# The opening of a two-block kernel: the loads on one queue with x between the conditioning pieces, the first norm's root one chunk earlier

## The reference

```
c_act = silu(c)
mod = c_act @ w_ada[l] + b_ada[l]            # 1024 x 6144
sh_m, sc_m, gt_m, sh_f, sc_f, gt_f = split(mod, 6)
h = rms_norm(x, g_pre_mix[l]) * (1.0 + sc_m) + sh_m
y = mixing_sublayer(h, cos, sin, w_in[l], ...)   # proj = h @ w_in, rotary q and k, attention, pool
```

## Time and profile before

| what | value |
|---|---|
| median of 3 runs | 1512.08 us |
| lowest, highest | 1511.72, 1513.73 us |
| the profiled execution's own time | 1513.09 us |
| its span in the trace | 1511.3 us |
| PE busy | 1467.7 us, 97% of the span |
| DVE, ACT, POOL busy | 41%, 43%, 48% |
| mean granted TensorE clock | 0.983 of full |

### The profile page before, as it was taken

One profiled execution on the slowest core, in us unless ns is written; L12 is line 12 of the kernel. 1 busy time (PEld: TensorE's weight loads), 2 busy tenths in 40 slices (PEclk: granted clock), 3 DMA queues, 4 the chain that ended last, 5 costly groups with the idle time before them and its releaser, 6 DMA issues.

```text
span 1511.3 us, 19773 instructions
## 1 busy us (share of the span) xinstructions
PE 1467.7 (97%) x7614; PEld 1229.0 (81%) x7614; DVE 623.3 (41%) x911; ACT 646.3 (43%) x941; POOL 718.7 (48%) x612
## 2 busy tenths in 40 slices
PE   8999999999999999999989989999999999999996
PEld 7899977888888888888956788888887888887885
DVE  6878456333332111522046311432456656553002
ACT  4453455545444322322255443553435555554331
POOL 3555215545454554555422363445546645455452
PEclk8999999999999999999999989999999999999998
DMA  8764133232322233235211232222322232323321
GB/s 350 279 245 159 30 97 107 84 109 86 101 93 83 81 115 95 73 111 140 98 42 57 84 111 84 84 84 84 112 84 84 83 111 83 111 77 98 95 85 65
DMA packets 27963, 160.77 MB, mean 106 GB/s; under 512 B 4824, under 2 KB 5080, under 8 KB 13176
## 3 DMA queue, kind: packets, MB, share of 16 engines
q1 hardware_dynamic: 25248, 151.08, 29.0%
q10 hardware_dynamic: 2648, 8.75, 2.1%
HBM read 157.04 MB, written 2.78 MB: 106 GB/s over the span
## 4 chain that ended last, share of the span: by engine, by line
PE 69%; issue 10%; DVE 9%; POOL 9%; ACT 2%; DMA 1%; POOLq 0%; SPq 0%; DVEq 0%; ACTq 0%
PE ps L1747 60%; POOL WL L813 8%; DVE ps L1269 2%; DMA raw<-w_up_dram 1%; DVE dl L1373 1%; PE ps L1976 1%; DVE xT L1367 1%; DVE ps L1364 1%; PE ps L1995 1%; PE ps L2008 1%; DVE rope L1439 1%; PE ps L1893 1%; PE ps L1928 1%; PE ps L1915 1%; POOL WL L775 1%
## 5 line engine op out<-in xcount | busy, mean ns | idle before, releaser
L775 POOL TENSOR_TENSOR WL<-raw,WH 128x512 fp32r<-128x512 f32 (+2 forms) x336 | 359.5, 1098 | 454.0 <-ACT WH L896 453.7
L1747 PE MATMUL ps<-hH,WH 128*128 128x512 f32 x1024 | 406.4, 397 | 0.9 <-POOL WL L813 0.9
L1747 PE MATMUL ps<-hH,WL 128*128 128x512 f32 x1024 | 399.6, 390 | 0.0
L1747 PE MATMUL ps<-hL,WH 128*128 128x512 f32 x1024 | 399.4, 390 | 0.0
L813 POOL TENSOR_TENSOR WL<-raw,WH 128x512 fp32r<-128x512 f32 x176 | 246.6, 1432 | 222.0 <-ACT WH L1064 222.0
L896 ACT ACTIVATE WH<-raw 128x1024 fp32r<-128x1024 f32 (+3 forms) x168 | 143.4, 882 | 220.4 <-PE ps L1747 207.2
L1747 PEld LDWEIGHTS ps<-hH,WH 128*128 128x128 f32 x1024 | 192.6, 188 | 46.0 <-issue 5.6
L1747 PEld LDWEIGHTS ps<-hH,WL 128*128 128x128 f32 x1024 | 192.6, 188 | 40.3
L1747 PEld LDWEIGHTS ps<-hL,WH 128*128 128x128 f32 x1024 | 192.8, 188 | 38.4
L1747 PE MATMUL ps<-hidH,WH 128*128 128x512 f32 x352 | 137.6, 391 | 1.1 <-POOL WL L813 1.1
L1747 PE MATMUL ps<-hidH,WL 128*128 128x512 f32 x352 | 137.0, 389 | 0.0
(11 more groups left out here) (300 smaller groups left out, 2311.2 us busy)
## 6 DMA issues: line engine op xcount, KB each, us to landing
raw<-w_up_dram SPq DMA_DIRECT2D x44, 1024.0 KB, 4.9
raw<-w_in_dram SPq DMA_DIRECT2D x36, 1024.0 KB, 4.9
adaw<-w_ada_dram SPq DMA_DIRECT2D x24, 1024.0 KB, 7.1
raw<-w_down_dram SPq DMA_DIRECT2D x16, 768.0 KB, 4.2
raw<-w_down_dram SPq DMA_DIRECT2D x16, 640.0 KB, 3.9
xT<-x_dram ACTq DMA_DIRECT2D x2, 2048.0 KB, 9.4
raw<-w_mem_kv_dram SPq DMA_DIRECT2D x4, 1024.0 KB, 4.7
raw<-w_out_dram SPq DMA_DIRECT2D x4, 1024.0 KB, 4.7
```

What stands on the lines that cost most here:

```text
L775: pool.tensor_tensor(WL[:, d % 2, ks, cols], raw[:, d % 2, ks, cols], WH[:, d % 2, ks, cols].bitcast(F32), ALU.subtract).then_inc(lo_done, 1)
L1747: mm = pe.matmul(out, lhs[x], rhs[y], start=(first and i == 0), stop=(last and i == 2))
```

## The change

Three things are edited, all of them ahead of the second `apply` of the first norm.

1. *Queues.* x goes from ACT's queue to SP's, between pieces 1 and 2 of w_ada. The positions and the row of frequencies go from the head of SP's queue to ACT's, behind `vec`. The mask table and `w_pool` go from ACT's queue to SP's, behind piece 7. The first two weight units are loaded together behind piece 3, instead of behind pieces 3 and 4.
2. *Conditioning.* The whole of chunk 2 comes after the first `apply` (before, its first half came ahead of it).
3. *The root and the idle matmuls.* The norm's root stands in front of the split of unit 0 on ACT; DVE waits for the spread reciprocal in `apply`, not in `norm`. The 57 matmuls on ones are 48 at the start and 9 behind the squares, ahead of `ada_turn` 1 on PE.

```diff
-        steps = [("start",), ("angles",), ("silu",), ("trig",), ("warm", 57), ("ada", 0), ("ada", 1), ("ada", 2, 0)]
+        steps = [("start",), ("angles",), ("silu",), ("trig",), ("warm", 48), ("ada", 0)]
         steps += [("squares", N_PRE1, k) for k in range(KD // 2)] + [("ada_turn", 0)]
-        steps += [("squares", N_PRE1, k) for k in range(KD // 2, KD)] + [("split", 0), ("ada_turn", 1), ("norm", N_PRE1), ("split", 1, 0)]
-        steps += [("ada_end", 0), ("keep_on", 8), ("apply", N_PRE1, 0, 4), ("split", 1, 1), ("ada", 2, 1), ("ada", 3)]
+        steps += [("squares", N_PRE1, k) for k in range(KD // 2, KD)] + [("warm", 9, None, 4), ("ada", 1), ("ada_turn", 1)]
+        steps += [("norm", N_PRE1), ("split", 0), ("split", 1, 0)]
+        steps += [("ada_end", 0), ("keep_on", 8), ("apply", N_PRE1, 0, 4), ("split", 1, 1), ("ada", 2), ("ada", 3)]
...
@@ sync
-            sp.dma_start(posi[:], a["positions"]).then_inc(pos_loaded, 16)
-            sp.dma_start(K[:, C_FREQ:], a["table"][:, P + C_FREQ:C_END]).then_inc(freq_loaded, 16)
-            for piece in range(4):
+            ada(0)
+            ada(1)
+            sp.dma_start(xT[:], a["x"]).then_inc(x_loaded, 16)
+            ada(2)
+            ada(3)
+            load(0)
+            load(1)
+            for piece in range(4, 2 * ADA_FIRST):
                 ada(piece)
-            load(0)
-            ada(4)
-            load(1)
-            for piece in range(5, 2 * ADA_FIRST):
-                ada(piece)
+            sp.dma_start(K[:, 0:C_FREQ], a["table"][:, P:P + C_FREQ]).then_inc(k_loaded, 16)
+            sp.dma_start(wpool[:], a["w_pool"].rearrange("(m g) c d -> (g c) m d", g=2)).then_inc(wpool_loaded, 16)
...
@@ scalar, start
                 sc.dma_start(vec[:], a["vec"]).then_inc(vec_loaded, 16)
-                sc.dma_start(xT[:], a["x"]).then_inc(x_loaded, 16)
+                sc.dma_start(posi[:], a["positions"]).then_inc(pos_loaded, 16)
+                sc.dma_start(K[:, C_FREQ:], a["table"][:, P + C_FREQ:C_END]).then_inc(freq_loaded, 16)
                 sc.dma_start(ident_t[:], a["table"][:, C_ID:C_ID + P]).then_inc(ident_loaded, 16)
-                sc.dma_start(K[:, 0:C_FREQ], a["table"][:, P:P + C_FREQ]).then_inc(k_loaded, 16)
-                sc.dma_start(wpool[:], a["w_pool"].rearrange("(m g) c d -> (g c) m d", g=2)).then_inc(wpool_loaded, 16)
...
@@ vector, norm and apply
-                ve.wait_ge(rstd_ready, i)
...
+                ve.wait_ge(rstd_ready, WHOLE[n] + 1)
...
@@ tensor
-            def warm(count, d=None):
+            def warm(count, d=None, bank=7):
```

More of the change, by code:

```diff
@@ L1725, in spread @@
                 mm.then_inc((ry_spread, rx_spread)[i], 1)
-            def warm(count, d=None):
+            def warm(count, d=None, bank=7):
                 pe.wait_ge(ones_ready, 1)
-                if d is None:
-                    bank = 7
-                else:
+                if d is not None:
                     bank = 0
```

## The result

| what | before | after |
|---|---|---|
| median | 1512.9 us (4 runs, 1511.72 to 1515.61) | 1526.51 us (4 runs, 1525.38 to 1527.68) |
| ratio to before, 95% interval | | 1.0084, 1.0071 to 1.0097 |
| profiled execution, span | 1513.09, 1511.3 us | 1525.38, 1523.6 us |
| PE busy, mean granted clock | 1467.7 us, 0.983 | 1477.2 us, 0.977 |

A forecast was written before the change was run, and what follows sets the result against it. PE is busy 97%, so DVE's chain of waits at the start sets the end. First `apply` from 28.8 to 35.4, +6.6 us (4.4 frequencies' landing, 2.2 PE's queue): median 1518.7 us, 8-in-10 range 1512.5 to 1521.

The forecast's parts named there:

- part 1: Load queues at the start: two queues take turns row by row, so the frequencies land 4.4 us later.
- part 3: Root and matmuls on ones: PE's nine matmuls hold turn 1 by 3.0 us; 2.2 us of the sum.
- F: Landing of the frequencies, 7.77 us before; forecast 12.2, with 11 and 13.2 as ends.
- S: Start of the second `apply`, 48.68 us before; everything behind it was taken as unedited, at no cost of its own.
- One for one: DVE's chain at the start: whatever delays it moves the end of the kernel by the same amount.
- PE's delay: Ahead of turn 1: squares and nine matmuls at the lower clock delay it 3.0 us (1.4 at the upper).
- A: Start of the first `apply`, comparable before 28.8 us; forecast 35.4, ends 33.7 and 36.9.
- the rival with the chance 0.06: Clock falls in PE's new gaps ahead of turns 2 and 3: 2 to 5 us on top, 1521 and more; chance 0.06.
- Part 2: Conditioning, chunk 2 moved behind the first `apply`: 3.3 us less ahead, 3.3 more behind, in the sum nothing.
- Nothing behind 48.68 is edited, and its parts all hang on this same chain: Kernel behind the second `apply`'s start: only shifts with DVE's chain, no further cost.
- turns of a whole load: Rival, load queues: frequencies land about 7.8 us as before; about 1512.5, no change; chance 0.15.
- small loads slip ahead: Rival, load queues: small loads pass before piece 0, frequencies land at 4 to 5 us; 1509.1 to 1511; chance 0.09.

The follow-up runs named there:

- e3: Kernel before with the changed steps (moved chunk, root, matmuls) but its own load order and queues; median 1516.63 us, ratio 1.0019.
- e9: Kernel before with only a delay: 26 small DVE instructions ahead of the angles; median 1519.16 us, ratio 1.0039.
- e2: Kernel before with only the new load queues, steps left as they were; median 1520.43 us, ratio 1.0042.
- e4: Changed kernel without the 9 matmuls on ones ahead of turn 1; median 1520.26 us, ratio 1.0051.
- e6: Changed kernel with 9 more matmuls on ones in PE's pause ahead of turn 3; median 1522.4 us, ratio 1.0049.
- e11: Changed kernel, unedited, profiled a second time; profiled execution 1525.24 us.
- e12: Changed kernel with `vec` issued at the head of SP's queue instead of ACT's; median 1516.85 us, ratio 1.0029.
- e5: Changed kernel with x sent behind piece 2 of w_ada instead of ahead of it; median 1520.95 us, ratio 1.0048.
- e1: Changed kernel with positions and frequencies back at the head of SP's queue, ahead of piece 0; median 1519.75 us, ratio 1.0041.
- e7: Changed kernel with positions and frequencies first on SP's queue, x directly behind piece 0, 9 matmuls added ahead of turn 3; median 1515.09 us, ratio 1.0009.

## Why the prediction was wrong in size

The forecast was slower by 6.6 us, and the span became 12.3 longer. The mechanism of part 1 held, and so did that of part 3; the sum was short by 5.7. Two of its terms failed: the first of the three that make F (`vec` beside piece 0, said to end at 5.05 and ended at 6.75), and all that lies behind S, which stood at nothing and cost 2.9 us.

1. *The landing of the frequencies*, forecast 12.2 (up to 13.2), measured 14.21: **2.0 us, of which 1.7 are in the first term** and 0.2 in the step down from 12.4 to 12.2. "`vec` beside piece 0, 9 x 0.37 = 3.3" from 1.75 us was to end at 5.05; `vec` landed at 6.75. The next two terms came as forecast, 2.55 us for the positions (2.6) and 4.9 for the frequencies (4.8). The start was too early in my estimate: 0.24 MB moved between 1 and 3 us, where I had a running queue's rate from 1.75 on. The prediction held the better number itself: it explained the 6.57 us of the earlier trace rows by 8 rounds "from about 3". With 3.0 in place of 1.75 the sum of 12.4 becomes 13.65. That reading of one execution was itself partly luck: with the same loads the frequencies took 6.57 us before, 5.9 in e3 and 4.2 in e9, less than eight rounds of 0.57. The cast was at 7.79, 7.15 and (before the delay) 5.52 in these, and at 13.8 to 14.3 in all five profiles with the new order on both queues and x behind piece 1 (the change, e2, e4, e6, e11). Against the earliest of the three the change moved the cast by 8.7 us, not by 6.45. e12 takes `vec` out of the way and gives back 7.65 us.
2. *One for one*: right up to S. e9 shows it with nothing edited but the delay.
3. *PE's delay*: from F to A, forecast 23.2 us, measured 23.66. The turn began 2.8 us late (forecast 3.0), so that the nine matmuls cost what was worked out; e4 gives back 2.5 of it. The turn and the spread then took 1.71 and 1.09 us where I had 1.05 and half of 1.09 beside `mod`: the clock was still at the lower level. `colA` stood blocked for 0.53 less 0.16 us (0.4; forecast 0.5). The Trainium skill, "SBUF — State Buffer", section "SBUF: two separate sides", makes this a matter of which instruction started first; the same instruction took 1.24 us in e9, 0.53 here and 0.16 in e2. The traces agree: it ended within 0.03 us of the end of a POOL instruction in e9 and here, and POOL had none running in e2.
4. *Part 2, chunk 2 behind the first `apply`, at nothing*: nearly. "I cost that at nothing because the matmuls of `keep_on` stand behind it" was wrong: behind the pause of 2.40 us the clock fell in the turn itself, and the matmuls of `keep_on` ran at the lower level, as did the first products. With 9 matmuls in the pause (e6) it did not fall; nor did it in e3 and e12, with nothing in it. It cost 0.2 us up to S by the marks (9.3 against 9.07 at A; 0.4 by e6) and 0.6 behind it. This was the rival with the chance 0.06; it happened, beside the forecast rather than in its place, at 0.8 to 1.0 us there and not 2 to 5.
5. *"Nothing behind 48.68 is edited, and its parts all hang on this same chain"* failed as a sum: another 1.5 us were lost between 103 and 108 us (0.4 up to the end of the wait for `hpL`, 1.1 in the clock's fall behind it) and 0.8 by the end, 0.6 of it behind 1091 us (the clock was low at 1138 to 1146, where before had none between 1080 and 1200). With the 0.6 these are 2.9 us, half of the miss. Why the clock fell there and not in the kernel before stays open; that a later start alone can bring it is shown by e9.

The sum: 6.6 + 2.0 + 0.5 + 0.2 + 2.9 = 12.2, of 12.3 measured. In the medians it is 13.6, since the first profile of before lies where its runs are and that of the changed kernel is the lowest of its four.

The rival "turns of a whole load" is out: rows at 99 to 99, 53 to 53 and 50 to 50, and e5. The Trainium skill, "DMA: Bandwidth & Descriptors", section "Queues, rings and completion order", has an engine take turns with packets of some 9 to 17 descriptors; under that the frequencies would land near 8 us, and they landed at 14.21. The rival "small loads slip ahead" is out, too, for this order: F was 14.21, not 4 to 5. In before's order something of it is seen in e9, where the frequencies needed only 4.2 us beside x.

The range ended at 1521. It had both ends of F and A but nothing for what lies behind S, where a term that stood at zero had only been argued for one pause. An honest upper end would have taken F at 13.2, A at its own end (36.9, and 1.0 more with that F), 1521.2 in the medians, and the lower end of the clock case on top, 1523; the measured time lies beyond that, too.

## What to carry to other kernels

When two queues are both busy, a small load costs the sum of the rows that stand opposite it, whatever its own size: put the load on which the first chain waits where nothing but small rows stands opposite, and count its rows from the end of a slow start, not from the issue. Work that is only there to keep the clock up must not stand in program order between a result and the instruction that waits for it. A shift of one engine's chain is one for one only until the next clock fall: a late start of 9.3 us cost 12.2 by the end. And before two halves of a change are added up, look whether each half has a wait that the whole has not, as piece 4 in e2 and unit 1 in e3.

## What the hardware showed that was not expected

- The first 2 us of the queues are slow and depend on what stands at their heads. From 2 to 7 us e1, with both small loads ahead of piece 0 on SP's queue, moved 256 GB/s, e12, with `vec` there, 391. Cause open.
- The same loads in the same order landed at different times: the 21 KB of frequencies took 6.57, 5.9 and 4.2 us in three profiles with before's loads. Cause open.
- Pauses of 2.40 to 2.42 us ahead of turn 3 were followed by a fall of the clock in four profiles and by none in two.
- An equal pause of PE (2.07 to 2.09 us, at 91 to 95 us) was followed by a clock of 1.00 in the kernel before and in e7, and of 0.55 in e12 a microsecond after PE had resumed:

```profile
94.00:96.00 2.00, 2.00 (x13) 2.00 (x12) 0.45 (x1) 2.00 (x4) 1.28 (x2) 0.55 1.04 438
```

  Each such fall costs 1.1 to 1.5 us in the marks behind it (1.1 in the changed kernel, 1.4 in e12, 1.5 in e9). It came in the same place in two profiles of the changed kernel. So the marks of one profile can differ by 1 to 3 us between two kernels for a reason that no edit names.
